# Hybrid decoder step: input projections as three-pass products, output gates in the gate stage, modulation behind all projections

## What is computed

```python
mod = silu(c) @ ada_w + ada_b                      # six vectors of D: sh1, sc1, gt1, sh2, sc2, gt2
hmix = rms(x) * (1 + sc1) + sh1
proj = hmix @ w_in                                 # D x 7960, split into
# q/k/v, z, b, a (gated DeltaNet) | q, f, i, g (HGRN2) | z, xbc, dt (SSD) | q, k, v, o, i, f (mLSTM) | 4 x D gates
out_a = rms(gated_delta(conv(qkv), ...)) * silu(g_z)
out_b = rms(hgrn2(...)) * silu(h_g)
out_c = rms((ssd(conv(xbc), ...) + d * x) * silu(s_z))
out_d = rms(mlstm(...)) * sigmoid(m_o)
merged = sum_n sigmoid(gate_n) * (out_n @ w_branch_n)
x = x + gt1 * (merged @ w_out)
x = x + gt2 * swiglu(rms(x) * (1 + sc2) + sh2)     # D_FF = 2816
return rms(x), final states of the four mixers
```

## Time and profile before

| | |
|---|---|
| median of 3 runs (lowest, highest) | 1296.57 us (1296.25, 1301.6) |
| profiled execution, its own time | 1298.08 us |
| its span | 1296.3 us |
| PE busy | 1209.0 us, 93% |
| PE weight loads busy | 1082.5 us, 84% |
| DVE busy | 549.6 us, 42% |
| ACT busy | 360.9 us, 28% |
| mean granted TensorE clock | 0.961 |

### The profile page before, as it was taken

One profiled execution on the slowest core, in us unless ns is written; L12 is line 12 of the kernel. 1 busy time (PEld: TensorE's weight loads), 2 busy tenths in 40 slices (PEclk: granted clock), 3 DMA queues, 4 the chain that ended last, 5 costly groups with the idle time before them and its releaser, 6 DMA issues. The chain is left out here.

```text
span 1296.3 us, 26018 instructions
## 1 busy us (share of the span) xinstructions
PE 1209.0 (93%) x11325; PEld 1082.5 (84%) x11325; DVE 549.6 (42%) x1116; ACT 360.9 (28%) x529; POOL 11.6 (1%) x29
## 2 busy tenths in 40 slices
PE   5599989989999999889999999969999999989997
PEld 3378767757777776889999998959999999989996
DVE  1351764566566744453333335462222222353322
ACT  2332371272212111552222221142222222341111
POOL 0000110000000000000000000000000000000000
PEclk9799999999998987989999999979999999989998
DMA  9812732023333031555333321312332332223201
GB/s 310 248 35 75 123 100 96 22 83 99 99 99 100 6 95 34 125 77 169 85 90 92 92 89 44 98 33 66 97 97 66 97 97 56 75 81 90 71 20 70
DMA packets 191030, 116.70 MB, mean 90 GB/s; under 512 B 36650, under 2 KB 189351, under 8 KB 190678
## 3 DMA queue, kind: packets, MB, share of 16 engines
q1 hardware_dynamic: 190358, 115.16, 32.2%
q0 software_dynamic: 576, 0.14, 0.1%
HBM read 108.31 MB, written 6.96 MB: 89 GB/s over the span
## 5 line engine op out<-in xcount | busy, mean ns | idle before, releaser
L746 PE MATMUL ps<-scr_parts 128*128 128x272 f32 x2688 | 521.7, 293 | 16.3 <-DVE hT_parts L2414 8.5
L746 PEld LDWEIGHTS ps<-scr_parts 128*128 128x128 f32 x2688 | 429.6, 191 | 20.3 <-issue 13.6
L746 PE MATMUL ps<-hT_parts,scr_parts 128*128 128x272 f32 x1408 | 391.3, 291 | 0.0
L746 PEld LDWEIGHTS ps<-hT_parts,scr_parts 128*128 128x128 f32 x1408 | 262.0, 190 | 0.0
L2316 DVE TENSOR_TENSOR scr_parts<-ring,scr_parts 128x1024 fp32r<-128x1024 f32 (+1 forms) x100 | 128.9, 1289 | 306.4 <-ACT scr_parts L1580 303.7
L746 PE MATMUL ps<-hT,ring 128*128 128x272 f32 x960 | 247.9, 410 | 3.0 <-ACT pj L1451 3.0
L1580 ACT ACTIVATE scr_parts<-ring 128x1024 fp32r<-128x1024 f32 (+1 forms) x100 | 111.0, 1111 | 490.1 <-PE ps L746 489.3
L746 PEld LDWEIGHTS ps<-hT,ring 128*128 128x128 f32 x960 | 182.5, 196 | 44.5 <-issue 3.9
L746 PE MATMUL ps<-pj_parts,scr_parts 128*128 128x272 f32 x992 | 168.8, 295 | 5.7 <-DVEq L1707 5.7
L746 PEld LDWEIGHTS ps<-pj_parts,scr_parts 128*128 128x128 f32 x992 | 142.8, 192 | 7.3 <-DVEq L1707 6.3
L746 PE MATMUL ps<-scr 64*64 64x64 f32 (+6 forms) x2336 | 86.0, 234 | 12.9 <-DVEq L1707 5.1
(11 more groups left out here) (307 smaller groups left out, 941.0 us busy)
## 6 DMA issues: line engine op xcount, KB each, us to landing
ring<-in_w_in_dram SPq DMA_DIRECT2D x62, 512.0 KB, 6.7
ring<-in_ada_w_dram SPq DMA_DIRECT2D x48, 512.0 KB, 6.6
ring<-in_ffn_w_in_dram SPq DMA_DIRECT2D x44, 512.0 KB, 5.0
ring<-in_ffn_w_out_dram SPq DMA_DIRECT2D x16, 384.0 KB, 3.6
ring<-in_ffn_w_out_dram SPq DMA_DIRECT2D x16, 320.0 KB, 4.2
ring<-in_w_out_dram SPq DMA_DIRECT2D x8, 512.0 KB, 5.4
x_scratch<-scr SPq DMA_DIRECT2D x1, 2176.0 KB, 13.4
Q<-x_scratch SPq DMA_DIRECT2D x1, 2176.0 KB, 10.9
```

The costliest lines, as they stand in the source:

```text
L746: return pe.matmul(out, lhsT, rhs, start=start, stop=stop, skip_group_check=True)
```

## The change

1. The mixer stage keeps 11 of the 15 groups (22 tiles of 128 columns) and computes them as three-pass products: a tile is four parts of 4 steps x 3 matmuls (`unit_part`). Its weights are split in two halves: ACT copies 128 x 512 to `wx_hi`, DVE writes the low part back over the slot (`weights_high`, `weights_low`). One `wx_hi` buffer per half: half 0 of the next tile waits until part 1 of this one is done, half 1 until part 3 is.
2. `hmix` itself is split as it is made: ACT writes the high part into the tiles of `pj` that hold z later, DVE the low part into `hT`. `s_w` becomes a three-pass product too, with two new stages (`s_whi`, `s_wlo`). The split of `hT` ahead of the gate stage goes; a copy of the high part by ACT stays.
3. The groups of the output gates (`Z_ORDER`: SSD z, DeltaNet z, HGRN2 g, mLSTM o; 8 tiles) become the first 8 products of the gate stage. The Exp of each branch norm follows its Ln at once; Silu and Sigmoid of z come behind all 8. LAG goes from 7 to 4, and lift product `j` stands behind product `8 + j + 4`.
4. The modulation units stand behind all projections in `SEQUENCE`; `turn` is one part. PSUM banks are waited for one by one (`BANK_FREE`).
5. SP loads z weights as the last four of the window, and all 16 gate loads stand behind the stores.

```diff
-MIX_ORDER = [0, 1, 2, 9, 10, 4, 5, 6, 11, 12, 13, 3, 8, 7, 14]
+MIX_ORDER = [0, 1, 2, 9, 10, 4, 5, 6, 11, 12, 13]
+Z_ORDER = [8, 3, 7, 14]
...
-LAG = 7
+Z_TILES = [2 * g + c for g in Z_ORDER for c in range(2)]
+LAG = 4
...
-for _n in range(len(MIX_ORDER)):
-    SEQUENCE += [("mix", 4 * _n + _v) for _v in range(4)]
-    if _n >= ADA_FROM:
-
-        SEQUENCE[-1:] = [("ada", _n - ADA_FROM), SEQUENCE[-1], ("turn", _n - ADA_FROM)] if _n - ADA_FROM < 8 else SEQUENCE[-1:]
+SEQUENCE += [("mix", _n) for _n in range(2 * len(MIX_ORDER))]
+for _n in range(8):
+    SEQUENCE += [("ada", _n), ("turn", _n)]
...
+            def three(out, wh, wl, hi, lo, start, stop):
+
+                mm(out, wh, hi, start, False)
+                mm(out, wl, hi, False, False)
+                return mm(out, wh, lo, False, stop)
...
                 if kind == "mix":
-                        last = mm(ps[:, u % 2, 0:HN], ring[:, n % R, at:at + P], hT[:, k, h * HN:(h + 1) * HN], k == 0, k == KD - 1)
+                    e, h = part_ // 2, part_ % 2
+                    if h == 0:
+
+                        pe.wait_ge(x_split, 2 * v + e + 1)
...
+                        last = three(ps[:, bank, 0:HN], wh[:, k % 4, :], wl[:, k % 4, :], x_hi[k][:, c], h_lo[:, k, c], k == 0, k == KD - 1)
...
+            def weights_high(i, e):
+
+                raw, _ = mix_weights(i, e)
+                n = load_of[("mixer", i // 2)]
+                landed(act, n % R, n)
+                if i and e == 0:
+                    act.wait_ge(x_half, i)
+                elif i:
+                    act.wait_ge(x_done, TILE_DONE[i - 1])
+                act.activation(mix_hi(e), raw, ACT.Copy).then_inc(x_split_hi, 1)
...
+            def weights_low(i, e):
+
+                raw, lo = mix_weights(i, e)
+                dve.wait_ge(x_split_hi, 2 * i + e + 1)
+                dve.tensor_tensor(lo, raw, mix_hi(e).bitcast(F32), SUB).then_inc(x_split, 1)
...
             for k in range(KD):
-                normalise(xT0, k)
+                if k + 1 < KD:
+                    normalise(xT0, k + 1)
+                dve.wait_ge(h_split_hi, k + 2)
+                dve.scalar_tensor_tensor(out=h_lo[:, k, 0:T], in0=hT[:, k, 0:T], scalar=mod[:, k, 0:1],
+                                         in1=x_hi[k][:, 0:T].bitcast(F32), op0=ADD, op1=SUB).then_inc(h_split, 1)
...
-            for k in range(4 * KD + LAG):
-                if k < 4 * KD:
+            for k in range(M_WOUT + LAG):
+                if k < M_WOUT:
...
-            low(0)
-            for k in range(KD):
-                dve.wait_ge(gate_in_hi, k + 1)
-                dve.tensor_tensor(h_lo[:, k, :], hT[:, k, :], h_hi[:, k, :].bitcast(F32), SUB).then_inc(gate_in, 1)
-            low(1)
+            for m in range(3):
+                low(m)
```

More of the change, by code:

```diff
@@ L263, in shared_order @@
     out, unit, part_, evac = [], 0, 0, []
+    mix_tiles = [u for u, (kind, _) in enumerate(SEQUENCE) if kind == "mix"]
+    split, stage_ = 1, 0
+    for e in range(2):
+        when[("lo", 0, e)] = 0.0
     left = {c: sum(cost(name, eng, t) + 0.1 for t, name, eng in stages) for c, stages in chains.items()}
@@ L292, in shared_order @@
         start, c, t, name, eng = best
-        if c == "x" and eng == "act":
+        if c == "x" and name == "read":
             free[eng] = start + 0.5
@@ L609, in _ @@
             sp.dma_start(hrow[64:68, 0:NB * 5:5], A["state_mlstm_m"][0].rearrange("b h -> h b")).then_inc(d_st, 16)
-            loads = window + [("gate", n) for n in range(R)]
+            loads = window + [("z", n) for n in range(R)]
             for n in range(8, len(loads)):
@@ L1627, in _ @@
-            for k in range(N_RAW, 4 * KD):
-                high(k + 2)
-                gate_out(k, ACT.Sigmoid)
-                if k >= 11 and k % 4 == 3:
-                    merged_high((k - 11) // 4)
+            for m in range(2):
+                high(m + 2)
+                z_out(m, ACT.Silu)
+            for m in range(2, M_GATE):
+                n = m - 2
+                high(m + 2)
+                z_out(m, ACT.Copy)
+                if n < 4:
+                    mid.begin(act, 0, f"o_rs{n}")
+                    for f in range(2):
+                        act.activation(two(rms[n][f]), ps[:, 4 + 2 * f:6 + 2 * f, 0:HN], ACT.Ln,
+                                       scale=1.0 / (P if n == 2 else DK), bias=colp[:, 3:4])
+                    act.drain().then_inc(mid_s, 1)
+                    for f in range(2):
+                        act.activation(rms[n][f], rms[n][f], ACT.Exp, scale=-0.5)
+                    act.drain().then_inc(rms_ready, 1)
@@ new lines, in _ @@
+            act.drain()
+            for z in (GZ, GZ + 1, HG, HG + 1):
+                act.activation(pj[:, z, :], pj[:, z, :], ACT.Silu).then_inc(z_ready, 1)
+            for z in (MO, MO + 1):
+                act.activation(pj[:, z, :], pj[:, z, :], ACT.Sigmoid).then_inc(z_ready, 1)
+            for k in range(4 * KD):
+                if k == len(GBUF):
+                    act.wait_ge(branch_ready, 1)
+                high(M_GATE + k + 2)
+                gate_out(k)
+                if k >= LAG + 4 and (k - LAG) % 4 == 0 and k < 4 * KD - 3:
+                    merged_high((k - LAG) // 4 - 1)
@@ L2298, in _ @@
             for chain, t, name, engine in order:
-                if engine == "dve":
+                if engine == "dve" and chain == "x":
+                    weights_low(t, int(name[-1]))
+                elif engine == "dve":
                     next(gens[chain])
```

274 lines of the change are left out of this document (165 added, 109 removed).

## The result

| | before | after |
|---|---|---|
| median (lowest, highest) | 1296.4 us (1295.7, 1301.6), 4 runs | 1337.7 us (1332.0, 1339.8), 4 runs |
| profiled execution, its span | 1298.1, 1296.3 us | 1338.7, 1336.5 us |
| mean granted TensorE clock | 0.961 | 0.916 |

After over before is 1.030 (95% interval 1.026 to 1.035): slower, as forecast, but by 41 us and not by 20. The measured 1337.7 us lies within the stated range, 1298 to 1338, by 0.3 us only.

What follows compares the result with a forecast made beforehand. PE was taken to set the pace in all stages, the mixer stage being full only through filling. Terms -21 (mixer stage), -1, +48.4 and -6.9 (gate stage) gave +19.5, say +20, from 1296.6 to 1317 us; range 1298 to 1338.

Steps and rivals of the forecast that it cites:

- -1, +48.4 and -6.9: Gate stage: the `hT` split goes (-1), eight more products (+48.4), the stall and half clock at the seventh product go (-6.9).
- Sum 293: Mixer stage from the end of `s_w` to the last filling part: 269 us of work and gaps plus two waits, ending at 374.
- 24 us were forecast for `s_ri` and late halves: Filled part of the mixer stage: 12 us of stall behind `s_ri` on DVE, 12 for other low halves arriving late.
- 117 + 10 = 127: Mixer stage behind the last filling part: 117 us with DVE at a share of 0.75, plus 10 for the clock.
- DVE's 88: Stretch without filling: DVE has 88 us of work, more than PE, so DVE is the larger.
- PE's 86 us: Stretch without filling: PE keeps 86 us of work once filling and the stages that come earlier are taken off.
- The 10 for the clock: Stretch without filling: half of it at half clock, PE's 43 us become some 75, a third on the path.
- The rival by which the clock stays up through short pauses: Stretch without filling: pauses of 1 to 3 us keep the clock, all else as forecast; 1307 us, chance 0.2.
- The mixer stage following PE: Mixer stage: chains have slack, so it loses all 87 us of moved PE work; 1250 us, chance 0.12.
- the starved one: Mixer stage: DVE at 0.65, half clock through the whole unfilled stretch, late halves at their upper end; 1340 to 1350, chance 0.1.
- The draw: Mixer stage: no clock loss, small early waits, DVE at 0.9 in the last stretch, saving 41 against 40.5; 1296, chance 0.12.
- the first rival: The mixer stage loses all 87 us of moved PE work, 1250; decided by an end before 481; chance 0.12.

Runs made afterwards that it cites:

- e_before_exp: The kernel before with each branch norm's Exp right behind its Ln, instead of all six behind the seventh high part; ratio 0.9954.
- e_load_dve: The changed kernel with one extra unused 128 x 128 DVE subtraction behind each of the 92 DVE stages after the last modulation part; ratio 1.0372.
- e_warm: The changed kernel with two extra unused 272-column matmuls behind every PE chain stage after the last modulation part; ratio 1.0485.
- e_noq: The changed kernel without 140 of the 160 matmuls of 4 columns in the sample tile; ratio 1.0190.
- e_one: The changed kernel with one of the three matmuls of each mixer-stage projection step, all splits kept; ratio 1.0027.
- e_late: The changed kernel with the eight modulation units held back, one behind every eighth or so chain stage from tile 2 of the gated DeltaNet on; ratio 1.0169.
- e_nolow: The changed kernel without the 44 low halves of the projection weights on DVE, the high part taken twice by PE; ratio 1.0258.

## Why the prediction was right and wrong

**Right: what bounds it, and the sign.** The gate stage has no cover for what is put there. Its terms were -1, +48.4 and -6.9, together +40.5; `w_out` starts 41.2 later. Behind its first product no PE wait is left in it, and `e_before_exp` shows the -6.9 nearly by itself: -6 in time (3 to 9), -4.2 in the gate stage of its profile. The stores of SP and ACT's table loads were hidden, as costed.

**Right: the start.** `s_w` ends at 81.0, forecast 80.5.

**Wrong: the mixer stage, forecast to end at 501 (-21), ended at 522.0 (0).** The failing term is "Sum 293: this part ends at 80.5 + 293 = 374". It took 309, to 390.0: 16 of the 21 us. The waits were not costed too low. 24 us were forecast for `s_ri` and late halves; the rows show 11.6 for low halves, 8.16 of them in one wait at 102.6. The sum's 107 us of chain stages and gaps, carried over from before, hold 17 us of PE's idle time (285.1 less 267.7 busy), so the 293 stood for 41 idle and 252 busy; measured are 37 idle and 272 busy. The 20 us are too much busy time. What the sum left out is the clock: it was costed in the stretch without filling alone, yet PE was busy at half clock for 53.8 us of the filled part, where the kernel before had 6.8. At full clock about half of the difference, 23 us, would not be there. That is an estimate from the pace of the earlier trace rows; no run had the filled part at full clock. In its favour, the three runs with the same order had 3 to 7 us less at half clock there than the changed kernel, and filled parts 1.5 to 2.6 us shorter. What brings the clock down in the filled part was not tested.

**Nearly right for partly wrong reasons: the stretch behind.** Forecast 117 + 10 = 127, measured 132. DVE's 88 was 86.8, at a share of 0.66 and not 0.75. But "DVE is now the larger" and so sets the pace did not hold: `e_load_dve` costs half of what it adds. PE's 86 us at full clock was too much, since 96.8 measured at a clock of 0.62 hold 71.7 at half speed, so about 61 at full. The 86 came from a row with 30.7 us at half clock and 5.9 of idle time, taken as full-clock work. The 10 for the clock was too small even by its own row: at the pace of the earlier trace rows 43 us of PE become 91 and not 75, and a third of the difference is 16. With 36 us from the clock, of which `e_warm` and `e_noq` put 0.5 to 0.8 on the path, the clock is worth 18 to 29 us there (an estimate: no run had this stretch at full clock), and without it the stretch would have been 103 to 114, shorter than the forecast's 117. So two errors nearly cancelled: that the term came out 5 us from the measured one is in part luck.

**The rule.** The rival by which the clock stays up through short pauses failed, and the prediction was right to keep a term against it: the clock was at half from 449.5 to 528 with no wait of PE above 3.1 us before the stretch's end, and in `e_warm` for 82 us with PE busy for 88% of them. That is against the Trainium skill, TensorE: Matmul & The Clock Gate, section "HAM oscillation — how this bites in real kernels", as the prediction had applied it. The Trainium skill's section "A second HAM failure mode: psum-queue depth-cycling" on the same page has a case in which many very short idle times of PE made the clock oscillate. That is nearer to these rows, but here the clock did not swing: it stayed at half, in `e_warm` with little idle time. The prediction's own reason, 4-column matmuls, fell with `e_noq`. What in this stretch keeps the clock down stays open; large matmuls that are close together, as in the gate stage, have it at 0.99.

**The rivals.** The mixer stage following PE was refuted by `e_one` too: even 89 us less of PE work gave back 36. The 1337.7 belongs to no case: it lies above the forecast's (1310 to 1328, a saving of 10 to 27 where the stage saved nothing) and just below the starved one (1340 to 1350), towards which it went by its half clock and not by its waits. Three sums of the rivals don't come out. The starved one's terms, 18 + 25 + 10 on 1317, are 1370. The draw's conditions, 10 us of early waits less, no clock loss and DVE at 0.9 (98 us), end the stage at 364 + 98 = 462 and not at 481, which is a time of 1278. And the first rival needs a stretch of under 107 us without a clock loss, not 97.

**The signs.** A wait of 8 us for a low half came (it ended at 102.6), as did PE at 7 tenths and a clock below 0.9 in the stretch. The last modulation part at 390, where 370 was forecast, DVE below 7 tenths and a gate stage that starts at 524 and not at 503 said that the mixer stage was costed too short.

**What was missed.** The change leaves a filled stretch in which PE is busy for 88% and an empty one behind it. `e_late`, which only moves some 20 us between them, ends the mixer stage at 501.6. That this is the forecast's number is chance, as it is another order. Holding filling back belongs to the work on the planner, whose greedy rule places each part as early as it can. Not tried: a second `wx_hi` buffer for each half, an order that takes both the low half and ACT's copy out from behind `s_ri`, and output gate products as filling.

## What to carry to other kernels

Filling is worth something only as long as a chain beside it would otherwise leave PE idle: when filling is made cheaper, spread what is left over the whole of the chains, rather than let a greedy order use it up early. Work moved out of a stage that is paced by chains is gained in part at most (none of 87 us here, 36 of 89 in `e_one`), and work moved into a stage that is paced by PE is paid in full, so cost the second exactly and prove the first. When a wait has two holders, taking one away only renames it (`e_nolow`): look at who releases the engine afterwards. Cost the clock over the whole stage, not only where PE looks idle.

## What was not expected of the hardware

The granted clock stayed at half for 78 us in a row (449.5 to 528) with PE busy at 70%. With two extra matmuls of 272 columns behind each stage, the clock still stood at half from 459.5 to the stage's end at 541.9, with PE busy at 88%. Taking out 89 us of projection work took the filled part's time at half clock from 61.5 to 119.5 us (0.90 to 0.78 in the mean), and busy time fell by 70 us and not by 89, at least in part for that.
